# Moving the last four modulation chunks between two layers, summing one norm wide, and splitting a scatter wait

## The reference, cut to what matters

```python
mod = jnp.dot(silu(c), w_mod[l]) + b_mod[l]            # c for the sample, c_ctx for the prompt
shift1, scale1, gate1, shift2, scale2, gate2 = jnp.split(mod, 6, axis=-1)
h = rms_norm(x, norm1_g[l]) * (1 + scale1) + shift1
x = x + gate1 * mixer(h)                               # layer 1: gated delta rule and grouped attention
h = rms_norm(x, norm2_g[l]) * (1 + scale2) + shift2
x = x + gate2 * expert_choice_ffn(h)                   # 16 experts, each takes its best 80 tokens
# rms_norm(x, g) = x * rsqrt(mean(x * x) + 1e-6) * g
```

## Time and profile before

| what | value |
|---|---|
| median of 3 runs | 1710.85 us (1703.96 to 1711.68) |
| the profiled execution | 1709.0 us, its span 1707.2 us |
| TensorE busy | 1571.3 us (92%) |
| VectorE, ScalarE, GpSimd busy | 39%, 25%, 15% |
| granted clock of TensorE, mean | 0.96 |
| read from HBM | 301.30 MB |

### The profile page before, as it was taken

One profiled execution on the slowest core, in us unless ns is written; L12 is line 12 of the kernel. 1 busy time (PEld: TensorE's weight loads), 2 busy tenths in 40 slices (PEclk: granted clock), 3 DMA queues, 4 the chain that ended last, 5 costly groups with the idle time before them and its releaser, 6 DMA issues.

```text
span 1707.2 us, 39998 instructions
## 1 busy us (share of the span) xinstructions
PE 1571.3 (92%) x17826; PEld 1034.9 (61%) x17826; DVE 667.8 (39%) x1414; ACT 426.9 (25%) x734; POOL 253.5 (15%) x263
## 2 busy tenths in 40 slices
PE   5999998989979999999999989988878998999996
PEld 2554434655546777766655558667666556767774
DVE  3543584751331111113039636644454134222221
ACT  3245413640311111113010236442232032000000
POOL 0000000000011111100000016155452001212211
PEclk8999999999989999997999989999999998999998
DMA  9444444025499999985121100002112617999995
GB/s 345 174 147 167 178 154 105 1 83 213 163 360 367 374 369 365 382 300 167 50 98 51 53 1 2 1 15 88 52 52 77 281 63 276 369 382 362 365 386 193
DMA packets 89932, 325.69 MB, mean 191 GB/s; under 512 B 11556, under 2 KB 17304, under 8 KB 81592
## 3 DMA queue, kind: packets, MB, share of 16 engines
q1 hardware_dynamic: 75824, 284.80, 44.3%
q0 software_dynamic: 9648, 32.65, 7.0%
q10 hardware_dynamic: 4312, 6.03, 1.0%
HBM read 301.30 MB, written 22.16 MB: 189 GB/s over the span
## 4 chain that ended last, share of the span: by engine, by line
PE 73%; DVE 7%; issue 3%; ACT 1%; DMA 1%; POOL 0%; POOLq 0%; DVEq 0%; ACTq 0%
PE pairs L225 19%; PE pairs L1648 17%; PE pairs L1660 7%; PE pairs L1665 3%; PE pairs L1631 2%; PE pairs L371 2%; PE pairs L1264 2%; PE pairs L2416 1%; PE pairs L2210 1%; PE pairs L2190 1%; PE pairs L1278 1%; PE pairs L2173 1%; PE pairs L1926 1%; PE pairs L762 1%; PE pairs L2427 1%
## 5 line engine op out<-in xcount | busy, mean ns | idle before, releaser
L225 PE MATMUL pairs<-hT,ring 128*128 128x128 f32 (+1 forms) x1120 | 306.1, 436 | 2.3 <-ACT hT L385 2.3
L225 PEld LDWEIGHTS pairs<-hT,ring 128*128 128x128 f32 x1120 | 170.6, 192 | 138.3 <-issue 138.2
L385 ACT ACTIVATE arena<-pairs 128x512 f32<-128x512 f32 (+6 forms) x214 | 124.7, 598 | 372.7 <-PE pairs L225 126.6
L1648 PE MATMUL pairs<-arena 128*64 128x80 f32 x5120 | 186.8, 235 | 9.7 <-issue 8.0
L1648 PEld LDWEIGHTS pairs<-arena 128*64 128x64 f32 x5120 | 181.7, 138 | 19.7 <-issue 17.2
L225 PE MATMUL pairs<-ring,hT 128*128 128x512 f32 (+1 forms) x448 | 178.5, 558 | 0.0
L225 PEld LDWEIGHTS pairs<-ring,hT 128*128 128x128 f32 x448 | 84.6, 191 | 90.3 <-issue 87.3
L1723 DVE TENSOR_TENSOR arena<-arena,pairs 128x160 f32<-128x160 f32 x64 | 20.6, 321 | 251.6 <-PE pairs L1648 251.6
L1648 PE MATMUL pairs<-arena,ring 128*64 128x80 f32 x3072 | 111.0, 233 | 5.8 <-issue 5.8
L1648 PEld LDWEIGHTS pairs<-arena,ring 128*64 128x64 f32 x3072 | 107.9, 137 | 12.1 <-issue 12.1
L385 DVE COPY arena<-pairs 128x512 f32<-128x512 f32 (+7 forms) x37 | 25.2, 703 | 127.5 <-PE pairs L225 120.8
(11 more groups left out here) (410 smaller groups left out, 2255.7 us busy)
## 6 DMA issues: line engine op xcount, KB each, us to landing
arena<-in_exp_w SPq DMA_DIRECT2D x60, 2048.0 KB, 18.8
ring<-in_exp_w SPq DMA_DIRECT2D x36, 2048.0 KB, 18.7
ring<-in_w_mod SPq DMA_DIRECT2D x22, 2048.0 KB, 8.1
ring<-in_w_in_ab SPq DMA_DIRECT2D x5, 2048.0 KB, 13.4
ring<-in_w_in_cd SPq DMA_DIRECT2D x5, 2048.0 KB, 7.9
ring<-in_w_out SPq DMA_DIRECT2D x4, 2048.0 KB, 15.2
h_rows<-arena POOLq DMA_DIRECT2D x10, 512.0 KB, 3.4
arena<-in_w_mod SPq DMA_DIRECT2D x2, 2048.0 KB, 10.0
```

Source lines behind the costliest of these rows:

```text
L225: last = pe.matmul(out, lhs(k), rhs(k), start=(k == 0), stop=(k == KD - 1))
L385: return eng.activation(dst, src, ACT.Copy) if eng is nc.scalar else eng.tensor_copy(dst, src)
L1648: last = pe.matmul(lin_of(j, f)[c:c + 64, :], w[:, k, f * P + c:f * P + c + 64], rhs, start=(k == 0), stop=(k == KD - 1))
```

## The change

Four things change.

- Chunks 20 to 23 move. Their loads stand ahead of layer 1's first projection chunk, in slots 6, 7, 8 and 0. Their matmuls, turns, copies and sums stand behind layer 0's experts in the ordinary form, ahead of the transposes; the fillers there drop from 12 to 4. The delta rule has no modulation work any more.
- The cache loads and the four loads of `rows_m` are issued by SyncE instead of ScalarE, behind projection chunk 4 and ahead of chunk 5. `rows_m` moves to another place of the arena.
- The first norm of layer 1 sums its squares the other way round: the ones are stationary and the squares move (512 and 128 columns), so that the sums come out on all partitions. The diagonals and the spreading matmuls go; the square root and the reciprocal now work on 128 x 640.
- In layer 1's experts GpSimd waits for the sample rows alone before their scatter, and for the prompt rows before theirs.

```diff
-                  ins[1] + all_mods[20:] + wouts[1]]
+                  all_mods[20:] + ins[1] + wouts[1]]
+        layer1_slots = [6, 7, 8, 0, 2, 1, 0, 2, 1, 0, 1, 0]
...
         def norm_root_act(act, l, n):
             ps = filled(act, ("nrm", l, n))
+            if (l, n) == (1, 0):
+                release(act.activation(rstd, ps[:, 0:T], ACT.Sqrt, scale=1.0 / D, bias=1e-6), ("nrm", l, n))
+                return
...
         def norm_rstd_dve(v, step, l, n):
             emptied(v, ("nrm", l, n))
+            if (l, n) == (1, 0):
+                step(v.reciprocal(rstd, rstd))
+                return
...
-                g.wait_ge(pair_free[3], base[3] + 2 * e + 2)
+                g.wait_ge(pair_free[3], base[3] + 2 * e + 2 - l)
...
                                          ye[set_of(e)][0:CAPS], None, compute_op=ALU.add).then_inc(room, 16)
+                    g.wait_ge(pair_free[3], base[3] + 2 * e + 2)
...
-                    if c == chunks[1][1]:
+                    if c == ins[1][1]:
+                        sum_rows_dma(sp, 0)
                         sp.wait_ge(S("m_quarter3"), 16)
...
-            keep_busy(pe, acc, 12)
+            for i in range(20, 24):
+                mod_rows_pe(pe, i, i % 2)
+                mod_turn_pe(pe, i, 2)
+            keep_busy(pe, acc, 4)
...
-                    for t in range(NT):
-                        last = pe.matmul(acc[:, t:t + 1], sq_all[:, j, t * P:t * P + P], ones[:, 0:1],
-                                         start=(j == t == 0), stop=(j == KD - 1 and t == NT - 1))
+                    for a, b in seg:
+                        last = pe.matmul(acc[:, a:b], ones, sq_all[:, j, a:b], start=(j == 0), stop=(j == KD - 1))
...
                     am(j + 2)
-                    late_mod_rows(pe, 20 + i, 0)
                     am(j + 3)
                     wu(j)
-                    late_mod_rows(pe, 20 + i, 1)
                     wu(j + 1)
-                    late_mod_turn(pe, 20 + i, late_row)
```

More of the change, by code:

```diff
@@ L271, in build @@
             loads.append((("experts", l), None, dict(last_in_slot)))
-            for s in range(3):
+            for s in SETS[2] + SETS[1]:
                 last_in_slot[s] = ("experts", l)
@@ L477, in build @@
         modsum = sm[:, 616:624]
-        mrow += [ar(25856 + 512 * i, 512) for i in range(2)]
-        mrow_of = lambda i: mrow[i % 2 + (2 if i >= 14 else 0)]
+        mrow += [ar(o, 512) for o in (25856, 26368, 11264, 11776)]
+        mrow_of = lambda i: mrow[i % 2 + (4 if i >= 20 else 2 if i >= 14 else 0)]
         MOD_RAW = 26944
@@ L717, in norm_scale_dve @@
                 emptied(v, x_unit(l, n, k))
-            emptied(v, ("nrb", l, n))
+            if (l, n) != (1, 0):
+                emptied(v, ("nrb", l, n))
             for k in range(KD):
@@ L1816, in load_stream @@
                             l = prev[1]
-                            pair = 1 + SETS[2].index(s)
-                            last = max(e for e in range(NE) if set_of(e) == 2)
+                            p = next(p for p in range(3) if s in SETS[p])
+                            pair = 1 + SETS[p].index(s)
+                            last = max(e for e in range(NE) if set_of(e) == p)
                             sp.wait_ge(pair_full[pair], moe_base[l][pair] + (last + 1) * PER[pair])
@@ L1827, in load_stream @@
                     sp.dma_start(chunk(c), src.rearrange("(k p) n -> p k n", p=P)).then_inc(w_here[s], 16)
-                    if c == chunks[1][2]:
+                    if c == ins[1][2]:
                         layer1_consts_dma(sp)
@@ L2817, in delta_dve @@
                         x_first(j + 2 + e)
-                    late_mod_dve(v, step, 20 + i)
             o_sum(v, 9, dscr3, 0)
@@ L2998, in _ @@
                 if l == 0:
-                    gather_sum_act(act, l)
+                    for i in range(20, 24):
+                        mod_act(act, i)
         @block.vector
@@ L3043, in _ @@
                 if l == 0:
+                    for i in range(20, 24):
+                        mod_dve(v, step, i)
                     residual_dve(v, step, l, "ms")
```

10 lines of the change are left out of this document (4 added, 6 removed).

## The result

| | before | after |
|---|---|---|
| median | 1709.55 us (6 runs, 1703.96 to 1711.68) | 1717.66 us (6 runs, 1712.85 to 1720.11) |
| ratio | | 1.0053, 95% interval 1.0034 to 1.0072 |
| the profiled execution | 1709.0 us, span 1707.2 | 1712.85 us, span 1711.0 |
| granted clock of TensorE, mean | 0.960 | 0.956 |

The changed kernel is slower by 0.5%, some 8 us, where 6.3 us of gain were forecast; 1717.66 lies outside the range of 1697 to 1713 and has the other sign. The profiled execution of after is the lowest of its six runs, so its profile shows 3.9 us of the 8.

The account below looks back on a forecast made before the run. TensorE, busy for 1571 of 1707 us, was taken to bound the kernel. Delta rule -7.4, between the layers +2.8 and end -1.7 sum to -6.3 us: 1704.6 from the median 1710.85, range 1697 to 1713.

Parts of the forecast that it names:

- the first term, -7.4 us: Delta rule: removing four chunks takes 4 x 1.59 us plus one 1.00 us first half off the chain, -7.4 us.
- +1.0 forecast up to the projection: Between the layers: sums end 0.9 us later, and root and reciprocal add 0.1 us.
- scatter of the last expert: End of layer 0's experts: issued at 762.7, takes 10.5 us on busy DMA engines, delaying the rows' issue to about 773.5.
- transposes start: Between the layers: at 782.0 instead of about 774.6, behind late chunks, fillers and 1.2 us for clock, losing 7.4 us.
- transposes and wide sums: Between the layers: eight tiles take 13.8 us at the full clock against 20.3 before, gaining 6.5 us.
- slow start of the projection: Layer 1's first projection: starts at the lower clock after over 5 us without TensorE work, +1.8 us.
- the landing of the chunks: SyncE's queue: 5.3 us per 2.1 MB at 393 GB/s, chunks landing at 757.4, 762.8, 768.1 and 773.4.
- The early rows: Rival between the layers: shorter wait, transposes from 778, no loss at the projection; 1698.8 us; chance 0.20.
- The low clock through the sums: Rival between the layers: eight tiles take 27.7 us, 13.8 more; 1718.4 us, 7.6 slower than before; chance 0.12.
- the rival by which the delta rule keeps its time: Delta rule: GpSimd or ScalarE becomes the next wait, only 2 of 7.4 us arrive; 1710.0 us; chance 0.15.
- The late expert weights: Rival at layer 0's last expert: five more queued transfers delay its weights, 4 us; 1708.6 us; chance 0.06.
- The end, -1.7,: Last two scatters: the first starts behind the sample rows and ends before the prompt rows are ready, -1.7 us.

Follow-up runs that it names:

- before with wide sums: Kernel before with the norm by wide sums and the sample rows' scatter ahead of the prompt rows': 1699.43 us, ratio 0.9951.
- the same with filler: Kernel before with wide sums and earlier scatter, plus 8 fillers instead of 2 ahead of layer 1's first projection: 1701.69 us, ratio 0.9965.
- before with narrow chunks: Kernel before with the late chunks' matmuls moving 64 columns instead of 512, all else unchanged: 1713.51 us, ratio 1.0027.
- before with wide sums and fillers: Kernel before with wide sums, earlier scatter, 8 fillers ahead of the projection and one filler per round before a chunk's first half: 1702.18 us, ratio 0.9971.
- rows from ScalarE: Changed kernel with the experts' sum rows and two small caches fetched from ScalarE's queue again: 1720.74 us, ratio 1.0088.
- filler at the norm: Changed kernel with 8 fillers instead of 2 between layer 1's first norm sums and the first projection: 1709.73 us, ratio 1.0026.
- one or two fillers a round: Changed kernel with one 128 x 512 filler per delta-rule round, 1705.01 us; with two, and 8 fillers instead of 2 ahead of the projection, 1706.69 us.
- the chunks' shapes as filler: Changed kernel with filler matmuls and transposes of the late chunks' shapes in their old delta-rule places, without copies, sums or loads: 1705.40 us, ratio 1.0006.
- after, again: Changed kernel, unaltered, measured again on the chip of a later group of runs: 1713.55 us, ratio 1.0030.

## Why the prediction was wrong

**The step that failed** is the first term, -7.4 us: "what TensorE does behind the turn needs nothing from the chunk". That is so for its data and its waits, and the rival that I set against it (GpSimd or ScalarE as the next wait) did not come: the waits for GpSimd grew only by the first halves, and with filler in the same places the delta rule is shorter, not longer. What the chunks gave to the delta rule was their columns. They were the only 512-column matmuls from 1118 to 1290, among 64 and 128-column ones, and the profile of before said so only by its PEclk of 1.00 in the earlier trace rows, which I read as a given of the place. The same prediction had seen 0.50 under the narrow sums and turned it into a gain; I asked for the clock of the stretches to which work was added, and not of that from which it was taken.

The lengths of the delta rule in all the profiles, in us, with its granted clock:

| in the delta rule | kernels | length | clock |
|---|---|---|---|
| the chunks, wide | before, twice; before with wide sums; the same with filler | 213.9, 216.8, 215.0, 212.9 | 0.98, 0.97, 0.95, 0.98 |
| the chunks, narrow | before with narrow chunks | 222.3 | 0.90 |
| the chunks and a filler a round | before with wide sums and fillers | 214.7 | 0.96 |
| nothing | after, twice; rows from ScalarE; filler at the norm | 216.9, 216.8, 216.8, 212.7 | 0.89, 0.89, 0.89, 0.92 |
| one or two fillers a round | two kernels | 209.8, 209.2 | 0.94, 0.95 |
| the chunks' shapes as filler | the same kernel twice | 208.1, 211.4 | 0.99, 0.97 |

Without the chunks the mean is 215.8 us, with them (first line) 214.6: +1.2 instead of -7.4. With filler in their place it is 209.6 over the last two lines. One thing stays open: the filler of the chunks' shapes stands on the chain with the same 1.00 and 0.59 us as the chunks, and its delta rule is still some 4.9 us shorter (209.7 against 214.6, each with 3 to 4 us of spread). So something in a real chunk beside its time on TensorE may cost, its copies, the wait of its turn or its loads. In the two profiles of before, 4.2 and 5.6 us of TensorE's idle time have no wait that the profile shows, against 0.4 with the filler, which would fit; but in the kernel with wide sums they are 0.3 at 215.0 us. That was not taken apart. Nor did a run show the delta rule at the full clock with neither chunk nor filler, so whether 7.4 us was the right price of the chunks' TensorE time is not shown.

The Trainium skill, "TensorE: Matmul & The Clock Gate", Part 1, section "What's actually happening", says that the throttled state is the default and activity releases it. By that rule taking work away can slow the rest down. The trace agrees: 3718 records at 0.89 were busy for 182.4 us, 3799 at 0.99 for 175.7.

**The clock over all runs.** Each run lists its mean granted clock, so this does not hang on single profiles:

| kernel | runs | mean clock | median us |
|---|---|---|---|
| before | 82 | 0.965 | 1707.4 |
| after, first | 6 | 0.954 | 1717.66 |
| after, again | 12 | 0.9575 | 1713.55 |
| before, narrow chunks | 12 | 0.956 | 1713.51 |
| chunks' shapes as filler | 12 | 0.968 | 1705.40 |
| one filler a round | 12 | 0.966 | 1705.01 |
| before, wide sums and scatter | 8 | 0.968 | 1699.43 |

Among the 82 runs of before alone, a clock lower by 0.001 goes with 0.87 us more. After has 0.0085 less over its 18 runs: 7.4 us, about the size of its loss. At the clock of before the changed kernel would then be within 1 us of it. That is a correlation, and its slope is from one kernel; the narrow chunks are the experiment on it.

**Between the layers, +1.0 forecast up to the projection.** In the profile it was +2.6; over seven profiles of changed kernels with the rows in SyncE's queue the mean is 43.4 us against 39.9 over two of before (43.44 and 39.87), so +3.6. (The kernel with narrow chunks has the code of before in this stage and took 37.8; with it the difference is 4.3.) By parts, in us from the start of the span or as lengths:

| step | forecast | measured in the profile of after |
|---|---|---|
| chunk 23 can start | 773.4 | 774.49 |
| scatter of the last expert | 10.5 us | 7.2 (760.92 to 768.11) |
| transposes start | 782.0 | 781.73 |
| transposes and wide sums | 13.8 at the full clock | 13.85 at 1.00 |
| reciprocal of 128 x 640 | 4.1 | 4.15 |
| end of sums to projection | 7.1 | 7.12 |
| slow start of the projection | +1.8 | +2.0 (1.9 to 2.6 elsewhere) |

All rows but the scatter are close, the absolute times in part by luck: the stage started at 760.70, 1.7 us earlier than in before. Measured from that start the sums end 2.4 us later than before, not 0.9. The term that was mis-sized is the landing of the chunks. From the last expert weight (749.7) to chunk 23 (774.4) it was 6.2 us a chunk, where the sum had 5.3. It had taken the 393 GB/s of the earlier trace rows for SyncE's queue alone, but that is the rate of all queues; from 761.6 to 769.0, between the landings of chunks 21 and 22, GpSimd's queue had 22% of the DMA engines' time. The stage became one of DMA: in each of the seven profiles TensorE waits for `in_w_mod`, and in two of them also for `moe_rows`. In the kernel with wide sums alone it takes 32.9 us: moving the chunks there costs 43.4 - 32.9 = 10.5 us. The prediction had 7.4 for it, the later transposes.

**The rivals.** The early rows did not come. The low clock through the sums did not come either: 1.00 from 774 to 798. A loss of clock was the right danger in the wrong place; I had it as a risk where wide matmuls were added, and it came where they were taken away. Of the rival by which the delta rule keeps its time, the time came true and the reason did not. The late expert weights did not come: the last expert ended at 760.7 without a wait for them.

**The end, -1.7,** was -1.7 (14.24 to 12.52, and 12.48 to 12.56 in all kernels that have the edit).

With the delta rule at +1.2 in place of -7.4 and +3.6 in place of +1.0, the sum is 1.2 + 3.6 + 2.0 - 1.7 = +5.1 us. The two comparisons gave 0.53% and 0.30%, 9 and 5 us. Of the 11.4 us between this and the forecast of -6.3, the delta rule is 8.6.

## What to carry to other kernels

Before work is taken from a stretch of short matmuls, ask what holds the clock there: the wide matmuls that look like the cost may be what keeps the rest at 2.4 GHz, and one filler in a wait may be worth more than their removal. A moved block has two prices, at the old place and at the new; here the new place had 12 us of filler to replace on TensorE, but its loads came no sooner than the DMA engines let them, and the stage then waited for DMA. Test the parts of a change apart: the norm and the scatter were worth 0.5%, and moving the chunks, with the rows' queue, cost more than that, 0.8% on the same chip.

## What the runs showed of the hardware

- Less work, longer time: the same instructions in the same order with 64 instead of 512 columns in 64 of their records, and the kernel is 0.27% slower, with the granted clock at 0.90 instead of 0.97 and 0.98 in that stretch.
- Four fillers of 128 x 512 (one a round) moved the clock of 217 us from 0.89 to 0.94.
- Issuing a load can hold the issuing engine: three loads of 2 MB took 24.97 us to issue on SyncE, 17.60 of it the second, and four loads of 640 KB 8.23 on SyncE and 8.37 on ScalarE (2.71 in before, with the DMA engines partly idle). It is not the busy engines alone: with them as busy, the experts' weights of before took 0.33 to 0.38 us each, and the first loads on ScalarE's empty queue 0.34 to 0.46. An engine that issues loads and also copies for TensorE is then a wait for TensorE (4.34 us).
- While two queues shared the DMA engines they moved about as many packets each (281 and 279 from 773 to 775), and so the one with the smaller packets got less of the bytes (0.23 MB of 0.79).
- Profiles of one kernel differ by some 3 us in one stage (213.85 and 216.75 for one kernel, 208.14 and 211.35 for another).
